# Latent attention scores: two full passes and one of 32 rows for each key half, instead of three full passes

## The chip, the cores and the metric

The kernel runs on one core of a Trainium2 chip. The metric is the device time of the program in microseconds (us); lower is better. Of the kernel before, three runs are given: median 3897.62 us, lowest 3896.55, highest 3898.89.

The core has TensorE (matmuls and transposes, results into the banks of PSUM), VectorE, ScalarE and GpSimd (elementwise work; GpSimd can't reach PSUM here), and SyncE's queue, which issues most DMAs. In the rows PE is TensorE's matmul part, PEld its loading of stationary operands, DVE VectorE, ACT ScalarE, POOL GpSimd, SPq and ACTq the DMA-issuing queues.

## The reference, cut to what matters

The whole program is two transformer blocks in float32 on 1024 tokens: dilated attention, latent attention, then twice a mixer and a gated MLP. The change concerns the latent attention (mixer_mla), 16 heads, 64 channels without and 32 with rotary position:

```
q = (rmsnorm(cq, q_norm) @ w_uq).reshape(B, S, 16, 64 + 32)
q_nope, q_rope = q[..., :64], q[..., 64:]          # q_rope is rotated
kv = (rmsnorm(ckv, kv_norm) @ w_ukv).reshape(B, S, 16, 64 + 64)
k_nope, v = kv[..., :64], kv[..., 64:]             # k_rope is shared by the heads, and rotated
s = (q_nope @ k_nope.T + q_rope @ k_rope.T) * 96 ** -0.5
o = softmax(s) @ v
y = o * silu(gate)
```

## The kernel before, in words

**Precision.** TensorE's fast type for four-byte numbers (fp32r) keeps fewer bits than float32. So an operand x is held as a high part (x rounded to fp32r) and a low part (x minus the high part), and a product is three passes into one bank: high by high, high by low, low by high.

**Layout of a head.** Query and key channels lie on the 128 rows of SBUF, tokens on the 1024 columns. Rows 0 to 63 are the channels without rotary position. The rotation of the query is folded into the product: rows 64 to 95 hold the rotary channels, rows 96 to 127 the same channels with their halves exchanged, and the tile `msh` holds the factors of each row and token (scale, cosines, signed sines). The rotary key stands on rows 64 to 95 and again on 96 to 127, so that the matmul over 128 rows adds both. Buffers: `qh`, `ql` (high and low of the query), `kh`, `kl` (of the key), two of each, for even and odd heads. Rows 64 to 127 of `kh` and `kl` are the same for all heads and are filled once, in the step before (`act_latent`, `dve_latent`).

**The stage.** The heads are computed as 128 units: unit i is head i // 8 and the block i % 8 of 128 queries. Each engine has a written-out program of its own (`pe_heads` L2026, `act_heads` L2078, `dve_heads` L2127, `pool_heads` L1882), in which step i does parts of several units; engines meet only at semaphores, and each works its list strictly in order.

- TensorE, step i: in odd steps two transposes of the gate and 16 matmuls of probabilities by values for a pair of finished units (`bo`); 8 transposes of the probabilities of unit i-3; the scores of unit i; then one piece, if there is one. The scores are two key halves of 512 columns, three passes of 128 rows each, into two banks.
- ScalarE: the exponential with its sum (`act_head_exp`; odd step i: of unit i-1, first; even step: of unit i-1, after the copies), the copy of `bo` to `ml_o`, two copies of the transposed probabilities (high part), and in even steps the pieces of steps i-1 and i.
- VectorE: the sum into `ml_o`, two subtractions (low part of the probabilities, `ml_p`), the row maximum of unit i, the reciprocal of unit i-2, and in even steps the pieces.
- GpSimd: the low part of the query pieces (odd steps), the splitting of weight tiles into high and low (`split`: one CAST, one subtraction; a head's weights at i % 8 = 0, a tile of the output weights at i % 8 = 4 from step 40 on), the product of `ml_o` and gate (even steps from 6), and last the scaling of the gate by the reciprocal of unit i-3. TensorE's gate transposes of step i wait for the scaling of unit i-4.

**Pieces.** A head's query and key (halves q0, k0, q1, k1 of 512 tokens) are made while the head before is attended: in its steps i % 8 = 0 to 3. For even heads the values of two heads follow at i % 8 = 6 and 7. The pieces of head 0 stand ahead of step 0. A query piece goes: six passes on TensorE (`pe_piece`), the product with `msh` into the single buffer `ml_qs` on VectorE (`dve_piece`), which also frees the bank, rounding to `qh` on ScalarE (`act_piece`), subtraction to `ql` on GpSimd (`pool_piece_lo`). The next product waits until rounding and subtraction of the piece before are done. A key piece: three passes, rounding of rows 0 to 63 on ScalarE, subtraction on VectorE. Pieces and `bo` share two banks in turn (ring `o2`), the transposes have two (`t2`), the scores two pairs (`s2`). The scores of a head wait for both halves of its query's low part.

Line numbers of the trace for these calls are those of the helpers: L130 matmul, L133 transpose, L136 activation, L139 copy (CAST), L142 two-operand arithmetic, L145 arithmetic with a scalar, L153 maximum, L159 reciprocal.

Of the kernel before, what the change touches and what calls it, by code (L numbers as in the profile page):

```python
# [8 lines left out]
F32 = mybir.dt.float32  # L9
# [264 lines left out]
class Kernel:  # L274
# [13 lines left out]
    def layout(self):  # L288
# [95 lines left out]
        self.bjk, self.qg, self.kg = self.msc[:, 384:768], self.msc[:, 0:256], self.msc[:, 256:384]  # L384
# [5 lines left out]
        self.qh, self.ql = [self.thi[:, 2 * i, :] for i in range(2)], [self.thi[:, 2 * i + 1, :] for i in range(2)]  # L390
# [1355 lines left out]
    def act_latent(self, q):  # L1746
# [15 lines left out]
        def out(j):  # L1762
# [6 lines left out]
            q.activation(self.kh[0][64:128, blk(j)], kr, ACT.Copy)  # L1769
            q.activation(self.kh[1][64:128, blk(j)], kr, ACT.Copy)  # L1770
# [38 lines left out]
    def dve_latent(self, q):  # L1809
# [17 lines left out]
        def out(j):  # L1827
# [5 lines left out]
            kr = ps[64:128, b, 384:512]  # L1833
            for i in range(2):
                q.tensor_tensor(self.kl[i][64:128, blk(j)], kr, self.kh[i][64:128, blk(j)].bitcast(F32), ALU.subtract)
# [34 lines left out]
    def sp_heads(self, sp):  # L1870
        uq, ukv = self.I["b_w_uq"][0], self.I["b_w_ukv"][0]
        for h in range(16):
            pieces = []
            for k in range(2):
                r = uq[blk(k), h * 96:h * 96 + 96]
                pieces += [(k * 128, r), (k * 128 + 96, r[:, 80:96]), (k * 128 + 112, r[:, 64:80])]
            pieces.append((256, ukv[:, h * 128:h * 128 + 128]))
            if h % 2 == 0:
                pieces += [(384, ukv[:, h * 128 + 64:h * 128 + 128]), (448, ukv[:, h * 128 + 192:h * 128 + 256])]
            self.load(sp, ("head", h), pieces)  # L1880
# [91 lines left out]
    def act_piece(self, q, h, what, hf):  # L1972
# [3 lines left out]
        if what == "q":  # L1976
# [3 lines left out]
            q.activation(self.qh[x][:, r], self.qs[:], ACT.Copy).then_inc(*S.up("hi", key))  # L1980
        elif what == "k":
# [3 lines left out]
            q.activation(self.kh[x][0:64, r], p[0:64, :], ACT.Copy).then_inc(*S.up("hi", key))  # L1985
# [9 lines left out]
    def dve_piece(self, q, h, what, hf):  # L1995
# [3 lines left out]
        if what == "q":  # L1999
# [5 lines left out]
            q.tensor_tensor(self.qs[:], p, self.msh[:, r], ALU.mult).then_inc(*B.free(key, "evac_v"))  # L2005
# [12 lines left out]
    def pool_piece_lo(self, q, h, what, hf):  # L2018
        if what != "q":
# [3 lines left out]
        q.tensor_tensor(self.ql[x][:, r], self.qs[:], self.qh[x][:, r].bitcast(F32), ALU.subtract).then_inc(  # L2023
            *self.S.up("lo_p", ("hq", h, hf)))

    def pe_heads(self, q):  # L2026
# [3 lines left out]
        for i in range(128 + 4):  # L2030
# [22 lines left out]
            if i < 128:  # L2053
# [9 lines left out]
                for c in range(2):  # L2063
                    o, r = ps[:, b + c, :], half(c)
                    q.matmul(o, self.qh[x][:, blk(j)], self.kh[x][:, r], start=True, stop=False)
                    q.matmul(o, self.qh[x][:, blk(j)], self.kl[x][:, r], start=False, stop=False)
                    ins = q.matmul(o, self.ql[x][:, blk(j)], self.kh[x][:, r], start=False, stop=True)
# [1366 lines left out]
```

## Time and profile before

| | |
|---|---|
| median of three runs | 3897.62 us |
| profiled execution, its span (no other time of it is given) | 3899.6 us |
| TensorE, matmuls | 3734.7 us busy, 96%, 19015 instructions |
| VectorE | 2203.4 us, 57% |
| GpSimd | 1920.5 us, 49% |
| ScalarE | 1471.4 us, 38% |

The busy share of an engine is the sum of its instructions' time over the span; matmuls are pipelined and each is shown for longer than its distance to the next. The stage of the heads lies between about 870 and 1430 us of the span. In a timeline row stand: start (us from the span's start), duration (us, of all instructions that the row merges), engine, line, operation, output tile and input tiles, form, count, and in brackets the idle time of the engine just before, with what ended it. The names: `ml_qs` the query product, `thi` (several buffers under one name) the query's parts or the transposed probabilities' high part, `tfi` or `ml_e` the exponentials, `cst_sm` small statistics.

### The profile page before, as it was taken

What the parts mean: (1) busy time and instruction counts of PE and PEld (TensorE: products, weight loads), DVE (VectorE), ACT (ScalarE), POOL (GpSimd) and SP (SyncE); (2) the same over time, 40 slices, a digit from 0 to 9 for tenths busy, and PEclk for the clock granted to TensorE, in tenths of its full rate; (3) what the DMA queues carried; (4) which work ended last, traced back from release to release, by engine and by line L of the source; (5) the groups of instructions that cost most, each with busy time, mean ns of one, the idle gap of its engine ahead of it and who ended that gap; (6) DMA issues with size and microseconds to landing.
All of it is one profiled execution on the core that took longest, in us unless ns stands there. A gap on an engine that the chain in (4) does not pass through costs nothing.

```text
span 3899.6 us, 49530 instructions
## 1 busy us (share of the span) xinstructions
PE 3734.7 (96%) x19015; PEld 3088.3 (79%) x19015; DVE 2203.4 (57%) x3514; ACT 1471.4 (38%) x2954; POOL 1920.5 (49%) x1675
## 2 busy tenths in 40 slices
PE   6999999899999998999898999999999898999998
PEld 5888887887888877877687888887878587888887
DVE  4425254836777756544648777444444648777533
ACT  3224231326666653226544333222225534333211
POOL 3223223823333327221536888976221526778975
PEclk9999999999999999999899999999999999999999
DMA  5323222320000013110132222544110132222543
GB/s 182 96 83 92 81 67 85 107 78 15 6 12 6 9 37 102 61 30 7 33 131 78 81 84 79 200 145 138 49 36 17 33 125 73 84 84 87 180 161 124
DMA packets 244615, 309.84 MB, mean 79 GB/s; under 512 B 38085, under 2 KB 156245, under 8 KB 244378
## 3 DMA queue, kind: packets, MB, share of 16 engines
q1 hardware_dynamic: 211768, 231.86, 19.1%
q10 hardware_dynamic: 32610, 74.80, 5.5%
q8 instruction: 151, 2.47, 0.3%
q14 instruction: 86, 0.70, 0.1%
HBM read 252.96 MB, written 51.53 MB: 78 GB/s over the span
## 4 chain that ended last, share of the span: by engine, by line
PE 68%; DVE 12%; ACT 3%; issue 3%; POOL 1%; DMA 0%; ACTq 0%; SPq 0%; DVEq 0%; POOLq 0%
PE ps L130 64%; PE ps L133 3%; DVE ml_p L142 3%; DVE cst_sm L153 3%; ACT thi L136 1%; DVE f_ta L150 1%; DVE f_tb L150 1%; ACT ml_o L136 1%; DVE tlo L142 1%; ACT tfi L136 0%; POOL mlo_z L142 0%; DVE cst_sm L150 0%; DVE tfl L142 0%; POOL mix_z L142 0%; DMA wst<-in_w_in 0%
## 5 line engine op out<-in xcount | busy, mean ns | idle before, releaser
L139 POOL CAST whi<-wst 128x512 fp32r<-128x512 f32 (+2 forms) x508 | 423.9, 834 | 1241.2 <-DMA wst<-in_a_w_in 347.9
L142 POOL TENSOR_TENSOR wlo<-wst,whi 128x512 fp32r<-128x512 f32 (+2 forms) x634 | 936.2, 1484 | 40.8
L130 PE MATMUL ps<-whi,thi 128*128 128x512 f32 (+3 forms) x1816 | 710.1, 391 | 28.7 <-DVE tlo L142 10.8
L130 PE MATMUL ps<-whi,tlo 128*128 128x512 f32 (+3 forms) x1816 | 686.2, 378 | 0.0
L130 PE MATMUL ps<-wlo,thi 128*128 128x512 f32 (+3 forms) x1816 | 685.6, 378 | 0.0
L130 PEld LDWEIGHTS ps<-whi,thi 128*128 128x128 f32 x1816 | 345.2, 190 | 90.5 <-DVE tlo L142 11.9
L130 PEld LDWEIGHTS ps<-wlo,thi 128*128 128x128 f32 x1816 | 345.5, 190 | 57.7 <-issue 3.8
L130 PEld LDWEIGHTS ps<-whi,tlo 128*128 128x128 f32 x1816 | 344.6, 190 | 58.3
L130 PE MATMUL ps<-thi,whi 128*128 128x512 f32 x856 | 339.2, 396 | 23.2 <-DVE tlo L142 15.0
L130 PE MATMUL ps<-thi,wlo 128*128 128x512 f32 x856 | 336.0, 392 | 0.0
L130 PE MATMUL ps<-tlo,whi 128*128 128x512 f32 x856 | 335.9, 392 | 0.0
L153 DVE TENSOR_REDUCE cst_sm<-ps 128x1 f32<-128x1024 f32 (+7 forms) x256 | 246.2, 982 | 122.4 <-PE ps L130 122.4
L130 PEld LDWEIGHTS ps<-thi,whi 128*128 128x128 f32 x856 | 162.3, 190 | 60.1 <-issue 12.8
L136 ACT ACTIVATE thi<-ps 128x512 fp32r<-128x512 f32 (+2 forms) x258 | 141.1, 565 | 159.8 <-PE ps L133 154.9
L130 PE MATMUL ps<-mla_kh,thi 128*128 128x512 f32 x512 | 191.4, 414 | 1.9 <-ACT tfi L136 1.9
L150 DVE SCALAR_TENSOR_TENSOR f_tb<-f_ub,tfi,f_tb 128x1024 f32<-128x1024 f32 x88 | 190.7, 2167 | 1.6
L130 PEld LDWEIGHTS ps<-thi,wlo 128*128 128x128 f32 x856 | 162.4, 190 | 34.4
L130 PEld LDWEIGHTS ps<-tlo,whi 128*128 128x128 f32 x856 | 162.5, 190 | 33.0
L136 ACT ACTIVATE whi<-wst 128x512 fp32r<-128x512 f32 x126 | 70.5, 622 | 279.1 <-DVE wst L142 241.3
L142 POOL TENSOR_TENSOR tlo<-tfl,thi 128x512 fp32r<-128x512 f32 x96 | 152.3, 1592 | 6.1 <-ACT thi L136 1.1
L145 POOL TENSOR_SCALAR tfl<-tfl,cst_sm 128x64 f32<-128x64 f32 x128 | 56.7, 443 | 182.3 <-DVE cst_sm L159 176.1
L136 ACT ACTIVATE tfi<-ps,cst_sm 128x1024 f32<-128x1024 f32 (+1 forms) x112 | 119.3, 1066 | 50.2 <-DVE cst_sm L153 50.1
(393 smaller groups left out, 8103.9 us busy)
## 6 DMA issues: line engine op xcount, KB each, us to landing
wst<-in_w_down SPq DMA_DIRECT2D x140, 256.0 KB, 3.3
wst<-in_w_up SPq DMA_DIRECT2D x126, 256.0 KB, 2.9
scr_h<-f_tb SPq DMA_DIRECT2D x44, 512.0 KB, 3.9
wst<-in_w_in SPq DMA_DIRECT2D x80, 256.0 KB, 2.8
da_am<-in_ada_w SPq DMA_DIRECT2D x64, 256.0 KB, 2.7
wst<-in_a_w_in SPq DMA_DIRECT2D x72, 192.0 KB, 2.4
f_T2lw<-scr_h SPq DMA_DIRECT2D x48, 256.0 KB, 3.8
tfl<-scr_h SPq DMA_DIRECT2D x40, 256.0 KB, 3.8
```

The costliest lines, as they stand in the source:

```text
L130: return self.none if self.e is None else self.e.matmul(*a, **k)
L133: return self.none if self.e is None else self.e.transpose(*a)
L136: return self.none if self.e is None else self.e.activation(*a, **k)
L139: return self.none if self.e is None else self.e.tensor_copy(*a)
L142: return self.none if self.e is None else self.e.tensor_tensor(*a)
L145: return self.none if self.e is None else self.e.tensor_scalar(*a)
L150: return self.e.scalar_tensor_tensor(out=out, in0=a, scalar=s, in1=b, op0=o1, op1=o2, **k)
L153: return self.none if self.e is None else self.e.tensor_reduce(*a, **k)
```

## The change

The three products are arranged on fewer rows. A query piece is first summed over its two rotary row groups (rows 96 to 127 onto 64 to 95), so that 96 rows are left. Then, with n for the 64 rows without and r for the 32 rows with rotary position:

- pass 1: `q1` = [high n; low n] by `kh` = [high n; high n], 128 rows;
- pass 2: `q2` = [high n; high r; low r] by `kl` = [low n; high r; high r], 128 rows;
- pass 3: high r by low r of the key (`k3`), 32 rows. Of the first key half it uses rows 64 to 95 of `q2` and `k3`; of the second a copy of the query's rotary rows on rows 0 to 31 (even heads) or 32 to 63 (odd heads), with `k3` on the same rows. These two matmuls are the last of a unit, one behind the other.

For this VectorE gets an addition behind the product of a query piece, ScalarE rounds it twice (to `q1`, 64 rows; to `q2`, 96 rows), GpSimd makes two subtractions and a copy instead of one subtraction, and has waits ahead of them. The key piece's weight columns are loaded twice (one more DMA for each head), and its rounding covers 128 rows. In the step before, the rotary key's high part goes to `kl`, its low part to `k3`. A scratch tile (`bjk`) moves.

```
-            q.activation(self.kh[0][64:128, blk(j)], kr, ACT.Copy)
-            q.activation(self.kh[1][64:128, blk(j)], kr, ACT.Copy)
+            q.activation(self.kl[0][64:128, blk(j)], kr, ACT.Copy)
+            q.activation(self.kl[1][64:128, blk(j)], kr, ACT.Copy)
...
-            for i in range(2):
-                q.tensor_tensor(self.kl[i][64:128, blk(j)], kr, self.kh[i][64:128, blk(j)].bitcast(F32), ALU.subtract)
+            kr, krh = ps[64:96, b, 384:512], self.kl[0][64:96, blk(j)].bitcast(F32)
+            for r in (64,) if j < 4 else (0, 32):
+                q.tensor_tensor(self.k3[r:r + 32, blk(j % 4)], kr, krh, ALU.subtract)
...
-            pieces.append((256, ukv[:, h * 128:h * 128 + 128]))
+            pieces += [(256, ukv[:, h * 128:h * 128 + 64]), (320, ukv[:, h * 128:h * 128 + 64])]
...  (act_piece)
-            q.activation(self.qh[x][:, r], self.qs[:], ACT.Copy).then_inc(*S.up("hi", key))
+            q.activation(self.q1[x][0:64, r], self.qs[0:64, :], ACT.Copy)
+            q.activation(self.q2[x][0:96, r], self.qs[0:96, :], ACT.Copy).then_inc(*S.up("hi", key))
...
-            q.activation(self.kh[x][0:64, r], p[0:64, :], ACT.Copy).then_inc(*S.up("hi", key))
+            q.activation(self.kh[x][:, r], p, ACT.Copy).then_inc(*S.up("hi", key))
...  (dve_piece)
-            q.tensor_tensor(self.qs[:], p, self.msh[:, r], ALU.mult).then_inc(*B.free(key, "evac_v"))
+            q.tensor_tensor(self.qs[:], p, self.msh[:, r], ALU.mult).then_inc(*S.up("v_seq"))
+            q.wait_ge(*S.last("v_seq"))
+            q.tensor_tensor(self.qs[64:96, :], self.qs[64:96, :], self.qs[96:128, :], ALU.add).then_inc(*B.free(key, "evac_v"))
+            q.wait_ge(*S.last("evac_v"))
...  (pool_piece_lo)
-        q.tensor_tensor(self.ql[x][:, r], self.qs[:], self.qh[x][:, r].bitcast(F32), ALU.subtract).then_inc(
-            *self.S.up("lo_p", ("hq", h, hf)))
+        q.wait_ge(*self.S.last("w_lo"))
+        if h or hf:
+            q.wait_ge(*self.S.last("b_gate"))
+        q.tensor_tensor(self.q1[x][64:128, r], self.qs[0:64, :], self.q1[x][0:64, r].bitcast(F32), ALU.subtract).then_inc(
+            *self.S.up("p_seq"))
+        q.wait_ge(*self.S.last("p_seq"))
+        q.tensor_tensor(self.q2[x][96:128, r], self.qs[64:96, :], self.q2[x][64:96, r].bitcast(F32), ALU.subtract).then_inc(
+            *self.S.up("p_seq"))
+        q.wait_ge(*self.S.last("p_seq"))
+        if h == 1 and hf == 0:
+            for j in range(8):
+                q.wait_ge(*self.S.at(f"ld_g{j}"))
+        q.tensor_copy(self.q_third(h)[:, r], self.qs[64:96, :]).then_inc(*self.S.up("lo_p", ("hq", h, hf)))
+        q.wait_ge(*self.S.last("lo_p"))
...  (pe_heads)
-                    q.matmul(o, self.qh[x][:, blk(j)], self.kh[x][:, r], start=True, stop=False)
-                    q.matmul(o, self.qh[x][:, blk(j)], self.kl[x][:, r], start=False, stop=False)
-                    ins = q.matmul(o, self.ql[x][:, blk(j)], self.kh[x][:, r], start=False, stop=True)
+                    q.matmul(o, self.q1[x][:, blk(j)], self.kh[x][:, r], start=True, stop=False)
+                    q.matmul(o, self.q2[x][:, blk(j)], self.kl[x][:, r], start=False, stop=False)
+                q.matmul(ps[:, b, :], self.q2[x][64:96, blk(j)], self.k3[64:96, :], start=False, stop=True)
+                ins = q.matmul(ps[:, b + 1, :], self.q_third(h)[:, blk(j)], self.k3[self.third(h), :], start=False, stop=True)
```

## Rows read from the trace of the kernel before

**Rows 1.** Busy time in a stretch of the stage (PE, PEld, DVE, ACT, POOL; clock).

```profile
1114.00:1148.00 34.00, 33.28 (x224) 29.54 (x224) 24.04 (x42) 22.17 (x43) 12.74 (x18) 1.00 0.01 4
```

**Rows 2.** Groups of instructions, 870 to 1430 us: busy, mean ns, idle before.

```profile
L142 POOL TENSOR_TENSOR thi<-ml_qs,thi 128x512 fp32r<-128x512 f32 x32 | 41.2, 1286 | 161.5 <-ACT thi L136 161.5
...
L142 DVE TENSOR_TENSOR ml_qs<-ps,mod_sh 128x512 f32<-128x512 f32 x32 | 21.7, 678 | 54.1 <-PE ps L130 53.8 <-POOL thi L142 0.3
...
L142 DVE TENSOR_TENSOR mla_kl<-ps,mla_kh 64x512 fp32r<-64x512 f32 x32 | 21.3, 664 | 2.4 <-ACT mla_kh L136 2.4
```

**Rows 3.** Timeline of a pair without pieces in the ring.

```profile
1104.04 0.42 PEld L133 LDWEIGHTS ps<-cst_ident,ml_e 128*128 128x128 f32 x4 [0.56 <-DVE ml_p L142]
...
1106.88 1.21 DVE L153 TENSOR_REDUCE cst_sm<-ps 128x1 f32<-128x1024 f32 x1
...
1108.13 1.12 ACT L136 ACTIVATE tfi<-ps,cst_sm 128x1024 f32<-128x1024 f32 x1 [1.11 <-DVE cst_sm L153]
...
1109.36 0.59 ACT L136 ACTIVATE ml_o<-ps 64x512 f32<-64x512 f32 x1
...
1109.98 0.60 ACT L136 ACTIVATE thi<-ps 128x512 fp32r<-128x512 f32 x1
...
1111.81 1.21 DVE L153 TENSOR_REDUCE cst_sm<-ps 128x1 f32<-128x1024 f32 x1
...
1114.20 1.21 DVE L153 TENSOR_REDUCE cst_sm<-ps 128x1 f32<-128x1024 f32 x1
```

**Rows 4.** Timeline of the pair behind it, with one query piece.

```profile
1115.40 0.68 DVE L142 TENSOR_TENSOR ml_qs<-ps,mod_sh 128x512 f32<-128x512 f32 x1
...
1116.12 0.63 ACT L136 ACTIVATE thi<-ml_qs 128x512 fp32r<-128x512 f32 x1 [1.78 <-DVE ml_qs L142]
...
1116.65 1.10 ACT L136 ACTIVATE tfi<-ps,cst_sm 128x1024 f32<-128x1024 f32 x1
...
1118.49 0.42 DVE L142 TENSOR_TENSOR ml_o<-ps,ml_o 64x256 f32<-64x256 f32 x1 [2.41 <-ACT ml_o L136]
...
1122.75 1.21 DVE L153 TENSOR_REDUCE cst_sm<-ps 128x1 f32<-128x1024 f32 x1
```

**Rows 5.** Timeline of the next pair, with a key and a query piece.

```profile
1127.61 0.61 POOL L139 CAST whi<-wst 128x512 fp32r<-128x512 f32 x1
...
1129.51 1.21 DVE L153 TENSOR_REDUCE cst_sm<-ps 128x1 f32<-128x1024 f32 x1
...
1130.96 0.44 POOL L145 TENSOR_SCALAR tfl<-tfl,cst_sm 128x64 f32<-128x64 f32 x1 [0.39 <-DVE cst_sm L159]
1131.06 0.69 DVE L142 TENSOR_TENSOR ml_p<-ps,thi 128x512 fp32r<-128x512 f32 x1 [0.27 <-ACT thi L136]
...
1132.27 1.21 DVE L153 TENSOR_REDUCE cst_sm<-ps 128x1 f32<-128x1024 f32 x1
```

**Rows 6.** Timeline of a pair with value pieces, ScalarE.

```profile
1142.86 0.59 ACT L136 ACTIVATE ml_o<-ps 64x512 f32<-64x512 f32 x1 [0.41 <-PE ps L130]
```

**Rows 7.** Timelines of TensorE around 64-row pairs, from windows that begin at them.

```profile
1734.93 0.39 PE L130 MATMUL ps<-wlo,thi 128*128 128x512 f32 x1
1735.16 0.39 PE L130 MATMUL ps<-whi,tlo 128*128 128x512 f32 x1
1735.48 0.70 PE L130 MATMUL ps<-c_k,c_q 64*128 64x512 f32 x2
...
1736.01 1.02 PE L130 MATMUL ps<-c_k,c_q 64*128 64x512 f32 x4
...
1736.44 1.02 PE L130 MATMUL ps<-c_k,c_q 64*128 64x512 f32 x4
1737.40 0.29 PE L130 MATMUL ps<-cst_cmask,cst_idb 128*128 128x128 bf16 x2
```

**Rows 8.** Timeline of VectorE, 15 subtractions from SBUF behind the stage.

```profile
1428.75 9.11 DVE L142 TENSOR_TENSOR tlo<-tfl,thi 128x512 fp32r<-128x512 f32 x15
```

**Rows 9.** Timelines of VectorE and TensorE at the start of the stage.

```profile
870.74 0.69 DVE L142 TENSOR_TENSOR ml_qs<-ps,mod_sh 128x512 f32<-128x512 f32 x1 [53.64 <-PE ps L130]
...
877.56 0.45 PE L130 MATMUL ps<-mla_kh,thi 128*128 128x512 f32 x1
```

More of the change, by code:

```diff
@@ L383, in layout @@
         self.btmp = t.new("tmp", [128, 4, 16])
-        self.bjk, self.qg, self.kg = self.msc[:, 384:768], self.msc[:, 0:256], self.msc[:, 256:384]
+        self.bjk = self.place("ml2_jk", [128, 384], F32, mod + 81920)
+        self.qg, self.kg = self.msc[:, 0:256], self.msc[:, 256:384]
         t = Region(self, b + 16384, self.end, "ml3")
@@ L389, in layout @@
         self.qs = self.place("ml5_qs", [128, 512], F32, mod + 8192)
-        self.qh, self.ql = [self.thi[:, 2 * i, :] for i in range(2)], [self.thi[:, 2 * i + 1, :] for i in range(2)]
+        self.q1, self.q2 = [self.thi[:, 2 * i, :] for i in range(2)], [self.thi[:, 2 * i + 1, :] for i in range(2)]
+        self.q3 = self.place("ml5_q3", [128, 1024], F32R, b + 12288)
+        self.k3 = self.place("ml5_k3", [128, 512], F32R, mod + 10240)
         self.bp = [self.tfi[:, 4 + i, :] for i in range(3)] + [last[:]]
@@ L1832, in out @@
                     q.wait_ge(*S.at(f"st{i}", "a"))
-            kr = ps[64:128, b, 384:512]
-            for i in range(2):
-                q.tensor_tensor(self.kl[i][64:128, blk(j)], kr, self.kh[i][64:128, blk(j)].bitcast(F32), ALU.subtract)
+            kr, krh = ps[64:96, b, 384:512], self.kl[0][64:96, blk(j)].bitcast(F32)
+            for r in (64,) if j < 4 else (0, 32):
+                q.tensor_tensor(self.k3[r:r + 32, blk(j % 4)], kr, krh, ALU.subtract)
             q.tensor_tensor(self.cql[:, :, blk(j)], ps[:, b, 0:256].rearrange("p (a b) -> p a b", a=2),
@@ L2022, in pool_piece_lo, with third, q_third @@
         q.wait_ge(*self.S.at("hi", key))
-        q.tensor_tensor(self.ql[x][:, r], self.qs[:], self.qh[x][:, r].bitcast(F32), ALU.subtract).then_inc(
-            *self.S.up("lo_p", ("hq", h, hf)))
+        q.wait_ge(*self.S.last("w_lo"))
[12 more added lines that the diff above has]
+        q.wait_ge(*self.S.last("lo_p"))
+    def third(self, h):
+        return slice(32 * (h % 2), 32 * (h % 2) + 32)
+    def q_third(self, h):
+        return (self.q3 if h else self.thi[:, 7, :])[self.third(h), :]
     def pe_heads(self, q):
```

## The prediction, made before the changed kernel was run

> **What bounds the kernel now.** I read the page's busy shares first, then the granted clock, then the timeline of the attention heads, one unit (head and block of 128 queries) after another. The page says TensorE: 96% busy over the span, and 33.28 of 34 us in a stretch of that stage, with the upper of its two clock levels, 2.4 GHz, granted throughout (1.00) [rows 1]. The order of the work in the stage says otherwise. It has 128 units; the program goes through them in pairs, an even unit, then an odd one, and the start of the even unit's row maximum on VectorE marks a pair. Read by these marks, the eight pairs of two heads take 9.60, 9.54, 7.32, 7.32, 8.56, 9.53, 7.32 and 9.13 us, 68.3 in all, repeating to 0.02 us from head 2 to head 14; the 7.32, 8.56 and 9.53 can be taken from the marks in [rows 3 to 5].
>
> In a pair without pieces (7.32) the marks are 1106.88 and 1114.20 [rows 3]. Between them: maximum, exponential on ScalarE at 1108.13, copy of the output (ml_o) at 1109.36, copy of the transposed probabilities (thi) at 1109.98, two VectorE subtractions, the odd maximum at 1111.81, two more subtractions, the next mark. No step waits for TensorE; it is a ring of VectorE and ScalarE. TensorE waits for it instead: 0.56 us at 1104.04, for the subtraction that frees its bank. A shorter score block makes such waits longer, no more.
>
> In a pair with one query piece (8.56 = 7.32 + 1.24) the piece lies in the same ring: ml_qs on VectorE at 1115.40, its rounding on ScalarE at 1116.12, and only then, in ScalarE's order, the exponential at 1116.65 [rows 4]. In pairs with key and query piece it is the same ring, plus 0.38 us in which the second subtraction pair comes late behind TensorE (ScalarE's copy, then 0.27 us of VectorE wait at 1131.06; maximum to maximum 2.76 instead of 2.39) [rows 5]. Only the pair with value pieces (9.13) has TensorE ahead of ml_o [rows 6].
>
> **The change, part by part.**
>
> *TensorE, scores.* Per unit six passes of 512 columns become four and a pair of 32-row passes on disjoint rows, into two banks. Pitch of such a pass: 1735.16 - 1734.93 = 0.23 us [rows 7]. No 32-row pair is in the trace. The nearest are the 64-row pairs of the differential attention: two matmuls that both start at 1735.48 have ended 0.70 us later, and the next two start at 1736.01, where one after the other each would take the 0.43 between 1736.01 and 1736.44 [rows 7]: they run side by side. (These are of another type, 0.43 and not 0.23 us a pass.) I take the new pair as one pass. But those rows also show a price. From the last full-height matmul to the first pair it is 0.32 us instead of 0.23 (+0.09); from the first pair to the second 0.53 instead of 0.43 (+0.10); and 1736.44 to 1737.40, two pairs and the way back to full height, is 0.96 instead of 0.86 (+0.10). Sum: -0.23 + 0.09 + 0.10 + 0.10 = +0.06 us a unit; with a little for a slow first matmul behind it, +0.1 is my value, bounds -0.23 (no price) and +0.33 (no overlap, with the price). In the pair without pieces the last score pass ends as late as before (a step of 0.09 more, 0.23 less, a pass 0.1 longer), so the ring keeps its 7.32. With the value pieces two units count: 7 pairs x 0.2 = +1.4 us (bounds -3.2 and +4.6).
>
> The Trainium skill ("TensorEngine Tiling (Array Packing)", Key Properties) says that a change of tiling mode drains TensorE; its page "TensorE: Matmul & The Clock Gate", Measured speedup vs the span model, gives packed tiles a matmul's duration and about 4 ns for each further tile. The trace agrees with both: side by side, at a price on each side. By the second rule alone the scores would save a pass a unit, the value pairs would gain 3.2 us where I count a loss of 1.4, and the sum below would be 40.
>
> *VectorE and ScalarE, query piece.* After the multiplication VectorE now waits for itself and adds rows 96 to 127 onto rows 64 to 95, and only then releases ScalarE, which rounds twice (64 and 96 rows) instead of once. Fewer rows don't shorten these (kl's 64 rows take 0.66 us, ml_qs's 128 take 0.68) [rows 2]. The add: 512 elements from SBUF on VectorE take 9.11/15 = 0.61 us in a row of 15 [rows 8]; alone, with its start and the self-wait before it, I take 0.70. The second rounding: ScalarE's step from rounding to exponential, 1116.65 - 1116.12 = 0.53 [rows 4]. Together +1.23 us ahead of the exponential, in the ring: bounds 1.1 (0.61 and 0.5) and 1.4 (0.75 and 0.65). There are 32 pieces [rows 2], 30 inside the stage. Seven are alone in their pair: 7 x 1.23 = 8.6. Two in the first head, unpaced by TensorE: 2.5. In the other 21 the 0.38 us of lateness goes, as TensorE is then early: 21 x 0.85 = 17.9. Sum 29.0. What is late next is still the ring; ml_qs is single, but its next user comes 7 us later.
>
> *GpSimd, query piece.* One subtraction of 1.29 us [rows 2] becomes two and a copy of 0.61 (the CAST of rows 5), with self-waits: 3.4 us, +2.1, and starts later by the ring's 1.23. In most pairs GpSimd has over 2 us of waiting to absorb it. Behind the second query piece of a head, however, comes in 10 heads the splitting of an output weight tile (1127.61, then 1.3 us), then ml_o's product, and then the scaling of the gate at 1130.96 for which TensorE's next transposes wait. Laid out: piece 1127.15 to 1130.5, gate, split to 1132.85, product to 1133.7, gate scaled at 1134.15; TensorE would be there at 1132.85. It then ends the value products 2.3 us later, at 1136.5, where ml_o could begin at 1135.6. So 10 x 0.9 = 9 us (bounds 0 and 12).
>
> *Start of the stage.* The first head's pieces have no cover. Now ml_qs at 870.74, first scores at 877.56 [rows 9]. After, with the durations above: product and sum 1.4 us, two roundings to 873.2, GpSimd 3.4 us to 876.7, then the second ml_qs (which waits for GpSimd), rounding to 879.2, GpSimd to 882.65. Scores at 882.7: +5.1 us (bounds 2 and 8; a fall of the clock in TensorE's new idle time is in the upper one).
>
> *At nothing:* the key piece's copy of 128 rows for 64 (same duration); fewer subtractions in the latent step, under TensorE's gate matmuls; one more DMA a head on SP's queue, loaded two heads ahead; GpSimd's wait for the gate DMAs at head 1, issued 15 us before. Without their cover they are under a us each. No other stage changes.
>
> Sum: 29.0 + 1.4 + 9 + 5.1 = +44.5. The profiled execution has no own time beside its span of 3899.6; the median of the runs is 2.0 lower. 3899.6 + 44.5 - 2.0 = 3942. As the GpSimd term is the least sure of a laid-out chain, I take it at half: 3938.
>
> **Rivals.**
> (a) *TensorE is the bound, as its 96% say*: each unit saves a pass, 128 x 0.23 = 29 us: 3868, faster. For it: the page, and 2.76 against 2.39 in 21 pairs. Against it: the ring's rows, in which no step of a 7.32 pair waits for TensorE. It decides only if the ring had slack that the rows don't show. Chance 0.06.
> (b) *The additions hide*: VectorE's wait of 2.41 us before ml_o's sum [rows 4] takes them up, TensorE is a wash, the start costs its 2 to 5: about 3900. Against it: that wait is for ScalarE, whose queue holds the rounding and the exponential, the ring itself. Chance 0.07.
> (c) *Ring lengthened, GpSimd and start absorbed*: 29.0 + 1.4 + 2: 3930. Same sign; chance 0.27.
> (d) *The 32-row passes don't overlap* (the promised saving doesn't come): +0.33 us a unit. Score ends then pass VectorE's readiness by about 0.2 in the odd-even step of 64 pairs, +13, and the value pairs +4.6: 44.5 + 13 + 3: 3958. Against it [rows 7]. Chance 0.12.
>
> **How the numbers follow.** The forecast (all terms, GpSimd in part to whole: 3932 to 3950) has 0.48; likeliest time 3938. A measurement of this kernel tells 0.2%, 7.8 us, from no change. The range leaves out (a), (b) and the far end of (d): 3912 to 3958. Faster: (a) and a little of (b), 0.07. Within: most of (b), 0.05. Slower: 0.88.
>
> **What would show it.** Marks of pairs without pieces still 7.32 apart; of the lone query pair 9.8; of key and query pairs 10.4 with the odd-even step at 2.39. Between ml_qs and the exponential 2.5 us instead of 1.25. The two 32-row passes start within 0.01 us, with 0.32 before them. TensorE's waits in the stage grow, although its busy time falls. A GpSimd wait of over 1 us before the value products in heads 5 to 14. First scores 5 us later after the first ml_qs. The forecast is wrong if the pairs without pieces get shorter than 7.32, or if the query pairs stay at 8.56.

## The result, and the profile after

The changed kernel takes 3949.4 us (median of 4 runs, 3947.2 to 3952.0) where the kernel before takes 3898.3 beside it: a ratio of 1.0133, interval 1.0120 to 1.0145. That is 51 us slower; the forecast was 3938, the range 3912 to 3958. The direction and the range held. The sum behind them did not hold in three of its terms.

The head of the page after (engine, busy us, share of the span, instructions):

```profile
span 3945.4 us, 49752 instructions
PE 3758.3 (95%) x19015; PEld 3052.3 (77%) x19015; DVE 2236.7 (57%) x3542; ACT 1490.9 (38%) x2986; POOL 1976.6 (50%) x1739
```

Busy time in the stage, from the first query product to the last row maximum; first line the kernel before, second the kernel after (stretch, its length, then PE, PEld, DVE, ACT, POOL with instruction counts; clock; DMA):

```profile
870.74:1414.29 543.55, 520.82 (x3362) 449.40 (x3360) 386.19 (x661) 363.51 (x663) 185.60 (x269) 1.00 0.04 11
```

```profile
868.74:1470.24 601.50, 555.82 (x3362) 423.03 (x3360) 406.64 (x693) 383.02 (x695) 246.40 (x333) 0.98 0.04 10
```

The stage is 58.0 us longer. TensorE issues the same 3362 matmuls in it; the time in which none ran goes from 22.7 to 45.7 us. Its busy time grew too, by 35 us: the scores of a unit take it 0.18 us longer (shown below), which is 23 us in 128 units, and part of the stage runs at the lower clock level (0.98 on the mean).

Groups of the stage after that answer to [rows 2] (line, engine, operation, tiles, form, count; busy us, mean ns; idle time before and its cause):

```profile
L142 POOL TENSOR_TENSOR thi<-ml_qs,thi 64x512 fp32r<-64x512 f32 x32 | 41.1, 1283 | 202.2 <-ACT thi L136 202.2
L142 POOL TENSOR_TENSOR thi<-ml_qs,thi 32x512 fp32r<-32x512 f32 x32 | 41.0, 1282 | 2.5
L142 DVE TENSOR_TENSOR ml_qs<-ml_qs 32x512 f32<-32x512 f32 x32 | 22.0, 686 | 1.1
L139 POOL CAST ml_q<-ml_qs 32x512 fp32r<-32x512 f32 x30 | 18.1, 602 | 2.0
```

Fewer rows cost the same: 1283 ns for 64, 1282 for 32, 1286 for 128 in [rows 2].

The timeline of a lone query piece after, which answers to [rows 4] (start, duration, engine, line, operation, tiles, form, count, idle time before):

```profile
1141.61 1.21 DVE L153 TENSOR_REDUCE cst_sm<-ps 128x1 f32<-128x1024 f32 x1
...
1143.01 0.69 DVE L142 TENSOR_TENSOR ml_qs<-ps,mod_sh 128x512 f32<-128x512 f32 x1
...
1143.73 0.69 DVE L142 TENSOR_TENSOR ml_qs<-ml_qs 32x512 f32<-32x512 f32 x1
...
1144.45 1.15 ACT L136 ACTIVATE thi<-ml_qs 64x512 fp32r<-64x512 f32 x2 [2.70 <-DVE ml_qs L142]
...
1145.51 1.10 ACT L136 ACTIVATE tfi<-ps,cst_sm 128x1024 f32<-128x1024 f32 x1
1145.69 2.66 POOL L142 TENSOR_TENSOR thi<-ml_qs,thi 64x512 fp32r<-64x512 f32 x2 [4.56 <-ACT thi L136]
...
1147.42 0.42 DVE L142 TENSOR_TENSOR ml_o<-ps,ml_o 64x256 f32<-64x256 f32 x1 [3.00 <-ACT ml_o L136]
...
1151.56 1.21 DVE L153 TENSOR_REDUCE cst_sm<-ps 128x1 f32<-128x1024 f32 x1
```

From the product to the exponential it is 2.50 us (1145.51 - 1143.01) where [rows 4] have 1.25. The maxima are 9.95 apart.

TensorE around a 32-row pair after, which answers to [rows 7]:

```profile
1140.55 0.40 PE L130 MATMUL ps<-mla_kl,thi 128*128 128x512 f32 x1
1140.88 0.50 PE L130 MATMUL ps<-ml_k,thi 32*128 32x512 f32 x1
1140.88 0.50 PE L130 MATMUL ps<-ml_k,ml_q 32*128 32x512 f32 x1
1141.31 0.50 PE L130 MATMUL ps<-mla_cqh,whi 128*128 128x512 f32 x1
1141.65 0.39 PE L130 MATMUL ps<-mla_cql,whi 128*128 128x512 f32 x1
```

Both matmuls of the pair start together. The steps are 0.33 before the pair, 0.43 behind it and 0.34 behind the first full matmul, 1.10 in all from the last full pass to normal pace (1140.55 to 1141.65), where four steps of 0.23 would be 0.92. So a unit costs TensorE 0.18 us more than six full passes, not less. In the 128 units the median steps are 0.33 and 0.43 too.

Marks (even units' maxima, as the prediction reads them) in both kernels. The last column is the difference over the stage. The pairs are named here by what VectorE's list has in them, which sets two names of the prediction right: the 9.60 pairs, seven of its 21 "key and query" pairs, have a value and a query piece, and 15 of the 26 pairs of 7.32 us that it calls "without pieces" have a key piece, which leaves them at 7.32 all the same.

| pair of units | before | after | in all |
|---|---|---|---|
| first product to fourth maximum | 21.53 | 34.60 | +13.1 |
| lone query piece, 7 pairs | 8.56 | 9.95 | +9.8 |
| key and query piece, 14 pairs; value and query piece, 7 pairs | 9.53; 9.60 | 10.33; 10.39 | +16.7 |
| value piece alone, 7 pairs | 9.13 | 9.46 | +2.4 |
| key piece alone, with the output weight's split, 10 pairs (heads 5 to 14) | 7.32 | 8.65, two of them 10.0 | +16.0 |
| other pairs with a key piece alone or none | 7.32 | 7.32 | 0 |

Sum 58.0, the stage's 58.0. The rest of the program is 12 us shorter in the profiled execution, and 7 if the stage's 58.0 is set against the medians' 51.1.

Two readings of the kernel before belong beside this table. In its lone query pair (8.56) TensorE is busy for 8.55 of 8.55 us:

```profile
1114.20:1122.75 8.55, 8.55 (x56) 7.58 (x55) 5.93 (x12) 5.38 (x11) 2.89 (x4) 1.00 0.00 0
```

The same holds for its value pairs. In a key and query pair (9.53) TensorE waits once, for VectorE's subtraction of the key piece:

```profile
1056.38 0.44 PE L133 MATMUL ps<-cst_ident,tfl 128*128 128x128 f32 x2 [0.62 <-DVE mla_kl L142]
```

### The profile page after: what moved, and what is told of

Its sections match the earlier page's. It is cut to its first block, busy times and chain, and to the rows that moved or that the text cites. A ratio compares the mean times of both kernels' runs of the same rounds, so it can differ in the third digit from the quotient of the medians.

```text
span 3945.4 us, 49752 instructions
## 1 busy us (share of the span) xinstructions
PE 3758.3 (95%) x19015; PEld 3052.3 (77%) x19015; DVE 2236.7 (57%) x3542; ACT 1490.9 (38%) x2986; POOL 1976.6 (50%) x1739
## 4 chain that ended last, share of the span: by engine, by line
PE 76%; DVE 12%; ACT 5%; issue 3%; POOL 3%; DMA 1%; SPq 0%; ACTq 0%; POOLq 0%; DVEq 0%
PE ps L130 72%; PE ps L133 4%; DVE ml_p L142 3%; DVE cst_sm L153 2%; ACT thi L136 2%; DVE ml_qs L142 1%; ACT tfi L136 1%; ACT ml_o L136 1%; DMA tfi<-in_ada_w 1%; DVE f_ta L150 1%; DVE tlo L142 1%; DVE f_tb L150 0%; POOL thi L142 0%; POOL wlo L142 0%; POOL mlo_z L142 0%
## 5 line engine op out<-in xcount | busy, mean ns | idle before, releaser
L130 PEld LDWEIGHTS ps<-thi,whi 128*128 128x128 f32 x856 | 162.2, 190 | 58.6 <-issue 12.9
L142 POOL TENSOR_TENSOR thi<-ml_qs,thi 64x512 fp32r<-64x512 f32 x64 | 82.1, 1282 | 204.7 <-ACT thi L136 202.2
L150 DVE SCALAR_TENSOR_TENSOR f_ta<-f_ua,tfi,f_ta 128x1024 f32<-128x1024 f32 x88 | 138.6, 1575 | 4.8 <-ACT f_ta L136 3.1
```

Source lines behind the costliest of these rows:

```text
L130: return self.none if self.e is None else self.e.matmul(*a, **k)
L142: return self.none if self.e is None else self.e.tensor_tensor(*a)
L150: return self.e.scalar_tensor_tensor(out=out, in0=a, scalar=s, in1=b, op0=o1, op1=o2, **k)
```

## The experiments

### The parts one by one

**e1_pass**: the kernel before with the third pass as a 32-row pair (the rest of the third product is left out) and nothing else changed.

```
-                    ins = q.matmul(o, self.ql[x][:, blk(j)], self.kh[x][:, r], start=False, stop=True)
+                for c in range(2):
+                    g = slice(64 * (1 - c), 64 * (1 - c) + 32)
+                    ins = q.matmul(ps[:, b + c, :], self.ql[x][g, blk(j)], self.kh[x][g, half(c)], start=False, stop=True)
```

> The kernel before with the new form of the score passes alone: four passes of 128 rows and, as third product, a 32-row pass for each key half on disjoint rows (64 to 95 and 0 to 31), from the old buffers; the rest of the third product is left out. No added work on VectorE, ScalarE or GpSimd. Theory (the stage is a ring of VectorE and ScalarE, and the 32-row pair costs TensorE more than the pass it saves): pairs without pieces stay at 7.32 us, value pairs 9.13 to about 9.4, in all +2 to +5 us. Rival (TensorE is the bound and the added query work ate the gain): about -29 us, pairs shortened by 0.46.

Measured: ratio 1.0025 (1.0014 to 1.0036), +8.7 us, more than the 2 to 5 expected. The 7.32 pairs stay, value pairs go to 9.46, lone query pairs to 8.91, key and query pairs to 9.70. So the saving claimed for TensorE isn't there even alone. Its price of 0.18 us a unit lands in full, 0.35 a pair, where TensorE was busy throughout (value pairs and lone query pairs), and by 0.17 in the other query pairs. Prediction and expectation had counted it only in value pairs. No run leaves the third pass out altogether, so what a pass that is really saved would give stays unmeasured.

**e2_ring**: the kernel before with a second VectorE operation behind the product (a maximum of 32 rows with themselves) and the rounding in two halves.

```
+            q.wait_ge(*S.last("v_seq"))
+            q.tensor_tensor(self.qs[96:128, :], self.qs[96:128, :], self.qs[96:128, :], ALU.max).then_inc(*B.free(key, "evac_v"))
...
-            q.activation(self.qh[x][:, r], self.qs[:], ACT.Copy).then_inc(*S.up("hi", key))
+            q.activation(self.qh[x][0:64, r], self.qs[0:64, :], ACT.Copy)
+            q.activation(self.qh[x][64:128, r], self.qs[64:128, :], ACT.Copy).then_inc(*S.up("hi", key))
```

> The kernel before with the query piece's additions on VectorE and ScalarE alone: behind the product a 32-row, 512-column operation in place that leaves the values as they are (maximum with itself) with its self-waits, and the rounding in two instructions of 64 rows. Scores and GpSimd as before. Theory: +1.25 us in each of 30 query pieces, of which 0.38 to 0.45 is covered in 21: +29 us, and 2.5 at the start: +31. Lone query pair 8.56 to 9.8, key and query pairs 9.53 to 10.33. Rival (the loss is mainly TensorE's, through mode changes in 128 units): under +10.

Measured: 1.0100 (1.0085 to 1.0115), +38.9 us. Lone query pairs 10.02, key and query pairs 10.59 (value and query 10.66), and the start, to the fourth maximum, 31.50 instead of 21.53: 10 us of the 38.9. Its two roundings take longer than those of the change:

```profile
1148.63 0.67 DVE L142 TENSOR_TENSOR ml_qs<-ps,mod_sh 128x512 f32<-128x512 f32 x1
1149.34 0.69 DVE L142 TENSOR_TENSOR ml_qs<-ml_qs 32x512 f32<-32x512 f32 x1
1150.06 1.27 ACT L136 ACTIVATE thi<-ml_qs 64x512 fp32r<-64x512 f32 x2 [2.61 <-DVE ml_qs L142]
1151.36 1.12 ACT L136 ACTIVATE tfi<-ps,cst_sm 128x1024 f32<-128x1024 f32 x1
```

1.30 us from rounding to exponential (1150.06 to 1151.36), 1.06 after the change (1144.45 to 1145.51). By this 0.24 a piece, 7 us over 30 pieces, the ring's part of the change, with its part of the start, is about 32, an estimate. It is the main part.

**e3_pool**: the kernel before with GpSimd's work of a query piece as in the change: a copy and two subtractions instead of one subtraction, with their waits.

```
+        q.tensor_copy(self.ql[x][64:96, r], self.qs[64:96, :]).then_inc(*self.S.up("p_seq"))
...
+        q.tensor_tensor(self.ql[x][0:64, r], self.qs[0:64, :], self.qh[x][0:64, r].bitcast(F32), ALU.subtract).then_inc(
...
+        q.tensor_tensor(self.ql[x][64:128, r], self.qs[64:128, :], self.qh[x][64:128, r].bitcast(F32), ALU.subtract).then_inc(
```

> The kernel before with GpSimd's additions alone: a copy of 32 rows and two subtractions of 64 rows instead of one of 128, with the waits for itself. Theory: the start of the stage +4 us, and in 10 heads the gate's scaling behind the output weight's splitting comes late, by 0.5 us on the ring (less than the 1.33 in the changed kernel, since GpSimd starts 1.25 us earlier here): about +9 us. Rival (GpSimd's waiting of over 2 us absorbs all of it): 0 to +2.

Measured: 1.0037 (1.0024 to 1.0050), +13.7 us. The ten pairs go from 7.32 to 8.20, the others stay, and the start grows by 5.8 us (21.53 to 27.29). The expectation had 0.5 for the ten pairs. That 0.88 is near the prediction's 0.9 is luck, since the prediction's figure stands for the whole change, where the ring's additions delay GpSimd too and 1.33 came.

The three parts alone give 61 us, 54 without e2's dearer roundings, against 51: they add nearly up.

### GpSimd's late gate

**e4_late_split**: the kernel after with the splitting of the output weight tile behind the scaling of the gate.

```
-            if i % 8 == 4 and 40 <= i < 128:
-                self.split(q, ("wo", "b", n // 8, n % 8))
...  (scaling of the gate)
+            if i % 8 == 4 and 40 <= i < 128:
+                self.split(q, ("wo", "b", n // 8, n % 8))
```

> The changed kernel with the splitting of the output weight tile moved behind the gate's scaling in GpSimd's step. Theory: the ten pairs of 8.65 and 10.0 us fall back to 7.32, 16 us of the changed kernel's loss go: +35 against the kernel before. Rival (those pairs are late for another reason, a transfer or VectorE): no change, +51.

Measured: 1.0098 (1.0083 to 1.0113), 3936.5 us, 12.9 less than the kernel after, and 16.2 less in the stage. All ten pairs are at 7.32 again, every other pair as after. This is what it removes, in the kernel after:

```profile
1159.42 0.45 POOL L145 TENSOR_SCALAR tfl<-tfl,cst_sm 128x64 f32<-128x64 f32 x1
...
1159.81 0.61 POOL L139 CAST whi<-wst 128x512 fp32r<-128x512 f32 x1
...
1160.51 1.29 POOL L142 TENSOR_TENSOR wlo<-wst,whi 128x512 fp32r<-128x512 f32 x1
...
1161.97 0.73 POOL L142 TENSOR_TENSOR tfl<-ml_o 64x256 f32<-64x256 f32 x1 [0.17 <-DVE ml_p L142]
...
1162.79 0.92 POOL L145 TENSOR_SCALAR tfl<-tfl,cst_sm 128x64 f32<-128x64 f32 x2
...
1163.29 0.44 PE L133 MATMUL ps<-cst_ident,tfl 128*128 128x128 f32 x2 [1.63 <-POOL tfl L145]
...
1164.05 0.34 PE L130 MATMUL ps<-thi,ml_v 128*128 128x256 f32 x1
1164.19 0.41 PE L130 MATMUL ps<-ml_p,ml_v 128*128 128x256 f32 x1
1164.40 0.42 PE L130 MATMUL ps<-thi,ml_v 128*128 128x256 f32 x1
```

The scaling that the gate's transposes need stands behind the split and the product in GpSimd's list; TensorE waits 1.63 us. In this pair (10.0 us) something follows: the value products step 0.12 us apart until 1164.05 and 0.21 from 1164.19 on. The granted clock, by stretches, here and in one of the eight pairs of 8.65:

```profile
1160.00:1163.00 3.00, 1.66 (x9) 0.89 (x7) 3.00 (x5) 2.52 (x5) 2.65 (x4) 1.00 0.02 5
1163.00:1168.00 5.00, 4.71 (x27) 4.71 (x28) 1.18 (x4) 2.17 (x4) 0.78 (x3) 0.66 0.00 0
1203.00:1208.00 5.00, 4.37 (x32) 3.82 (x32) 2.21 (x6) 2.89 (x5) 1.67 (x4) 1.00 0.01 3
```

After the wait the clock went to its lower level of 1.2 GHz for a while, and the pair's further 1.35 us go with that. In all ten pairs TensorE waits 1.63 to 1.66 us before the gate's transposes; in the eight others the clock stayed at 2.4 GHz, and why these two and not those is open. The Trainium skill ("TensorE: Matmul & The Clock Gate", HAM oscillation — how this bites in real kernels) tells of long waits for DMA between bursts of matmuls, each of which throttles the PE again. Here the wait is for GpSimd and of 1.65 us, and the lower level followed in two of ten places, so a wait of this length does it sometimes and not always.

### Is there one ring or two

**e5_exp_first**: the kernel before with ScalarE's rounding of the query piece behind the exponential, and the late split.

```
+            if i % 2 == 1 and self.piece_at(i - 1) and self.piece_at(i - 1)[1] == "q":
+                self.act_piece(q, *self.piece_at(i - 1))
...
-                    if self.piece_at(n):
+                    if self.piece_at(n) and self.piece_at(n)[1] != "q":
```

> The kernel before with two moves of order and no change of the work: ScalarE rounds the query piece behind the copies of the next odd step, so behind the exponential instead of ahead of it, and GpSimd splits the output weight tile behind the gate's scaling. Theory (the query piece lies in the ring only because of ScalarE's order): it leaves the ring; query pairs fall from 8.56 and 9.53 to what TensorE needs, about 7.9 and 8.5; pairs without pieces stay 7.32. In all about -25 us, 3874. Rival (TensorE or another engine holds the query pairs just as tightly): under 5 us of gain.

Measured: 0.9994 (0.9984 to 1.0003), 3896.7 us. No gain in the pairs: 9.53 stays 9.53, the lone pairs stay at 8.53 to 8.57, and 14 pairs with a key piece alone go from 7.32 to 7.50. The start falls by 4.0 us (21.53 to 17.51), of which those 14 take back 2.5. The theory of a single ring through the query piece fell. In the lone pairs TensorE has no idle time, as in the kernel before, so it holds them by itself. What is late in a key and query pair of e5:

```profile
1115.84 1.22 DVE L153 TENSOR_REDUCE cst_sm<-ps 128x1 f32<-128x1024 f32 x1
...
1117.04 0.66 DVE L142 TENSOR_TENSOR mla_kl<-ps,mla_kh 64x512 fp32r<-64x512 f32 x1
1117.09 1.11 ACT L136 ACTIVATE tfi<-ps,cst_sm 128x1024 f32<-128x1024 f32 x1 [0.44 <-DVE cst_sm L153]
...
1117.76 0.44 PE L133 MATMUL ps<-cst_ident,tfl 128*128 128x128 f32 x2 [0.62 <-DVE mla_kl L142]
...
1120.15 0.60 ACT L136 ACTIVATE ml_o<-ps 64x512 f32<-64x512 f32 x1 [1.86 <-PE ps L130]
```

The exponential is early, at 1117.09, and of no use: ScalarE then waits 1.86 us for TensorE's value products, which waited 0.62 for VectorE's key subtraction to free the bank. This second ring (maximum, key piece, bank, value products, ml_o) is what holds the pair at 9.53; in the 9.60 pairs the value piece stands in the key piece's place.

**e6_exp_first_after**: the same edit on the kernel after.

> The changed kernel with the same two moves. Theory: its added 1.25 us for each query piece leave the ring too; query pairs 8.2 and 8.8 instead of 9.95 and 10.33, unless GpSimd's longer piece (3.3 us) delays the gate's scaling; with the start's loss of some 10 us left, -35 to -45 us against the changed kernel with the late splitting: about 3897 (3890 to 3910), so near the kernel before and some 20 us behind the kernel before with the moves. Rival (with the query work out of the ring the saved pass pays): below the kernel before with the moves.

Measured: 1.0216 (1.0201 to 1.0231), 3984.8 us, 88 us above the 3897 expected, and slower than e4 (3936.5) instead of faster. GpSimd's piece of 3.3 us now begins 4.94 us behind the query product (1155.87 to 1160.81 of its trace), and 6.22 behind the next (1165.19 to 1171.41), where the kernel after has 2.68 (1143.01 to 1145.69). The next gate scaling and the next query product wait for it, and the 15 pairs behind a head's second query piece grow from 7.32 to between 10.8 and 12.6. Part of that is the clock: it is 0.94 on the mean of the stage here, 0.99 in e4. A step that left one engine's path was still on another's.

**e7_exp_first_pass**: e5 with the 32-row pair of e1.

> The kernel before with the two moves and the new form of the score passes alone (four full passes and the 32-row pair; the rest of the third product is left out). Here TensorE is the bound in the pairs with pieces, so it is the place where a saved pass would pay most. Theory: the pair costs TensorE 0.18 us a unit more than the two passes it replaces: 62 units in 31 pairs, +11 us against the kernel before with the moves. Rival (the pair saves 0.23 us a unit where TensorE is the bound): -14 us against it.

Measured: 1.0013 (1.0004 to 1.0022), 3904.8 us, +8.1 on e5 where 11 were expected. The pairs with pieces are those of e1 to 0.02 us (8.92, 9.70, 9.78, 9.46): the 32-row pair costs the same with the other order. TensorE is idle in the key and query pairs, so the expectation's premise that it is the bound holds for the lone query and value pairs only.

**e8_serial**: e1 with both 32-row matmuls on rows 64 to 95, so that they can't run side by side.

```
-                    g = slice(64 * (1 - c), 64 * (1 - c) + 32)
+                    g = slice(64, 96)
```

> The kernel before with four full passes and two 32-row passes on the same rows (64 to 95) for both key halves, so that they can't lie side by side (the rest of the third product is left out). Theory (the pair on disjoint rows overlaps fully): 0.23 us a unit more than on disjoint rows, +14 us in the 31 pairs with pieces and some +5 in the others through late scores: about +28 us against the kernel before. Rival (the price in the pair is not overlap but the 32-row form itself): the same as on disjoint rows, +9.

Measured: 1.0061 (1.0046 to 1.0076), +25.9 us, 17 more than e1. Here the pair is 0.66 us from start to the next matmul (1100.83 to 1101.49 below) instead of 0.43:

```profile
1100.50 0.40 PE L130 MATMUL ps<-mla_kl,thi 128*128 128x512 f32 x1
1100.83 0.73 PE L130 MATMUL ps<-mla_kh,thi 32*128 32x512 f32 x2
1101.49 0.50 PE L130 MATMUL ps<-mla_cqh,whi 128*128 128x512 f32 x1
```

So the overlap of the change is real and worth one pass, 0.23 us a unit; the steps into and out of the 32-row form stay. This is the prediction's case (d), which it priced at 16 us above its own sum; here it is 17.

**e9_no_sum**: e4 without VectorE's sum. The rotary part of rows 96 to 127 is left out of the query.

```
...
-            q.wait_ge(*S.last("v_seq"))
-            q.tensor_tensor(self.qs[64:96, :], self.qs[64:96, :], self.qs[96:128, :], ALU.add).then_inc(*B.free(key, "evac_v"))
```

> The kernel after, with the output-weight split behind the gate scaling (as in e4_late_split), and without VectorE's sum of the two 32-row parts: the low part of rows 96 to 127 of the query is left out, and the gathering reads what is there. Theory: the sum (0.69 us of VectorE between the query sum and the two roundings) stands on the chain of each pair with a lone query piece, so those pairs fall by about 0.7 us (9.95 to 9.2); pairs with a key and a query piece fall less, since a second ring of the same pair (the maximum, the key piece on VectorE, the bank, the value products, their division) ends at about 9.7, so 10.33 to 9.7; with the start's five pieces this makes about -22 us against e4_late_split: 3914. Rival: the sum lies in time VectorE waits anyway; then all pairs stay and the time is that of e4_late_split, 3936.

Measured: 1.0052 (1.0037 to 1.0068), 3916.6 us. Lone query pairs 9.23 (from 9.95), key and query pairs 9.70 (from 10.33), the start 4.6 us less. The sum is on the path for its full 0.72 in the first, and in the second for 0.63, down to the 9.70 that e1 has without any of the ring's additions: the second ring's length with the 32-row pair in it.

**e10_k_first**: the kernel before with the key piece brought forward, on ScalarE ahead of the even step's exponential, on VectorE ahead of the maximum.

```
+                if self.piece_at(i - 1) and self.piece_at(i - 1)[1] == "k":
+                    self.act_piece(q, *self.piece_at(i - 1))
...  (dve_heads, ahead of the maximum)
+            if i % 2 == 0 and self.piece_at(i - 1) and self.piece_at(i - 1)[1] == "k":
+                self.dve_piece(q, *self.piece_at(i - 1))
```

> The kernel before, with the key piece's work brought forward alone: ScalarE rounds the key piece before the even step's exponential and VectorE subtracts it before the maximum; the query piece as before. Theory of two rings of nearly equal length in a pair with key and query piece (9.53 us): the second (maximum, key piece, bank, value products, division) is cut and the first (query sum, rounding, exponential, value products, division, next query sum) holds at about 9.15: 21 pairs by about -0.4, -8 us: 3891. Rival: one ring only, that of the query; then nothing falls, or the earlier key rounding delays the exponential and the time grows by up to 12 us.

Measured: 1.0010 (1.0001 to 1.0019), 3900.1 us where 3891 was expected, a miss on the whole. The pairs that had 9.53 fall to 9.09, near the 9.15 expected. So the two rings of that pair aren't quite equal: the second is 9.53, the first about 9.1. But each key piece now lies in the pair before: the 9.60 become 10.20 and the lone query pairs 9.15, which I had not counted (the 9.53 pairs lose one key piece and get the next), and two heads take 68.6 us instead of 68.3. The start grows by 1.2.

**e11_k_exp_first**: e10 and e5 together, both rings cut.

> The kernel before, with both rings cut: the key piece brought forward as in e10_k_first, and the query piece rounded behind the exponential with the output-weight split moved back as in e5_exp_first. Theory of two rings: each cut alone gives nothing or little, both together give what neither does: pairs with both pieces from 9.53 to about 8.9, lone query pairs 8.55 as they are, 21 pairs by about 0.6: -13 us, 3885. Rival: a third wait (the division's bank, or TensorE's own work) stands right behind; then under 3 us is gained.

Measured: 0.9982 (0.9974 to 0.9991), 3888.7 us beside 3896.3: 7.6 us, the one version faster than both kernels, by about as little as can be told. The pairs with 9.53 go to 8.71. Neither cut alone did that (9.53 in e5, 9.09 in e10). TensorE's wait for the key's subtraction is gone; what is left is 0.32 us for the gate:

```profile
1123.30 1.10 ACT L136 ACTIVATE ml_e<-ps,cst_sm 128x1024 f32<-128x1024 f32 x1
...
1123.69 0.67 DVE L142 TENSOR_TENSOR mla_kl<-ps,mla_kh 64x512 fp32r<-64x512 f32 x1
...
1123.96 0.44 PE L133 MATMUL ps<-cst_ident,tfl 128*128 128x128 f32 x2 [0.32 <-POOL tfl L145]
...
1124.29 1.20 DVE L153 TENSOR_REDUCE cst_sm<-ps 128x1 f32<-128x1024 f32 x1
```

The pairs that got the key pieces give back most of it (9.60 to 10.20, 8.56 to 9.15): over the pairs of the stage 2.7 us are left. The start gains another 4.0 us, and that is the same 4.0 that e5 has alone. So the pairs show both rings, but the 7.6 us of the whole are only in smaller part theirs.

### The start

**e12_keep_clock**: e4 with 37 unused matmuls of 512 columns among the first head's pieces.

```
+            n = {("q", 0): 2, ("k", 0): 4, ("q", 1): 3, ("k", 1): 12, ("v", 0): 4, ("v", 1): 12}[piece[1:]]
...
+            for k in range(n):
+                q.matmul(ps[:, b0, :], self.cqh[:, 0, blk(0)], self.cqh[:, 0, half(0)], start=True, stop=True)
```

> The kernel after with the output-weight split behind the gate scaling (as e4_late_split), and 37 matmuls of 512 columns whose result nobody reads, put among the first head's pieces so that TensorE is not left idle there. Theory: the granted clock at the start of the scores (0.50 to 0.74 in windows of 5 us between 875 and 900 us in the kernel after, 1.00 in the kernel before) falls because TensorE waited for the first pieces, and costs some 3 to 5 us; with TensorE kept busy the clock reads 1.00 and the time from the first query sum to the fourth reduction goes from 34.6 to about 31, the whole from 3936 to about 3932. Rival: the start's loss is the chain of pieces alone; then the stretch stays at 34.6 or grows by what the added matmuls delay.

Measured: 1.0105 (1.0091 to 1.0119), 3937.0 us, as e4, where 3932 was expected. The clock over the start (the number behind the five engines' busy times), first in the kernel after, then in e12:

```profile
875.00:880.00 5.00, 3.10 (x18) 2.91 (x19) 2.62 (x5) 2.29 (x5) 2.37 (x2) 0.74 0.29 53
880.00:885.00 5.00, 5.00 (x16) 3.56 (x16) 1.63 (x3) 0.66 (x2) 2.66 (x4) 0.50 0.25 43
885.00:890.00 5.00, 4.57 (x14) 2.87 (x12) 2.94 (x4) 1.56 (x3) 0.35 (x1) 0.74 0.27 53
```

```profile
880.00:885.00 5.00, 5.00 (x23) 3.70 (x22) 1.71 (x3) 0.58 (x2) 2.36 (x3) 1.00 0.29 53
885.00:890.00 5.00, 2.82 (x12) 1.58 (x10) 2.87 (x4) 2.90 (x4) 1.62 (x2) 1.00 0.28 54
890.00:895.00 5.00, 4.21 (x10) 2.63 (x11) 1.33 (x3) 2.33 (x5) 1.50 (x2) 0.54 0.00 0
```

The clock holds until 890 us; but between 885 and 890 TensorE is idle for 2.2 of 5 us, and behind that it falls. First product to fourth maximum is 33.7 us instead of 34.6; the first maximum came 0.35 later, the three maxima behind it took 1.3 less. The trace's clock records have the lower level for 7 us of this stretch in e12 and for 17 in e4 and in the kernel after. So the fall was put off and made shorter, not taken away: 10 us less of it gave back 1.3 us. What the rest of it costs stays open.

## Why the prediction was right or wrong, step by step

- *The ring, query piece* (8.6 and 17.9 forecast, 9.8 and 16.7 measured): right in its additions, half right in what held the pairs before. Product to exponential is 2.50 us, the forecast's 2.5. The sum takes 0.72 (0.70 taken), the second rounding 0.53 (0.53). The lone pair rose by 1.40, not 1.23: the product stands 1.40 behind the maximum (1141.61 to 1143.01) and not 1.20 (1114.20 to 1115.40 in [rows 3, 4]), because TensorE ends the piece later: its own price reaching the ring. The forecast read the lone pair of the kernel before as the ring of VectorE and ScalarE alone. It was a tie: TensorE is never idle in it and e1, which lengthens TensorE's work alone, lengthens it by 0.35, while e2's 10.02 less its additions of 1.48 gives 8.54 for the ring (an estimate). That the additions came in full is owed to this tie. Key and query pairs rose by 0.80 (0.85 forecast). That they rise by less than the lone ones was put down to 0.38 us in which the second subtractions come late behind TensorE; e5, e9, e10 and e11 show behind it a second ring, through the key piece and the bank, which held the pair at 9.53 while the ring of the query piece was about 9.1. The sizes fit: e10's 9.09 and the additions of 1.25 make 10.34 (10.33 measured), with e2's 1.48 it is 10.57 (10.59 measured). The number was right, its reason was half of the truth, and it matters: a cut in the query piece's ring (e5) gained nothing in any pair.
- *TensorE, the pair* (1.4 forecast): right in kind, too low in size. Taken +0.1 us a unit, measured +0.18: the step behind the pair is 0.43 us and the next again 0.34, so both the entry and the exit are paid behind the 0.33 ahead. In [rows 7] the exit showed as 0.10 only. Value pairs 2.4 us instead of 1.4, and in e1 another 6 us in the query pairs and the start, which the forecast had at nothing. Pairs without pieces 7.32, as said.
- *Marks of waiting*: TensorE's waits grew, as said; that its busy time falls was wrong, it rose by 35 us in the stage, 23 of them the 0.18 us in each of 128 units.
- *GpSimd*: the mechanism and its place were right, the size was not. 10 x 0.9, taken at half "as the least sure of a laid-out chain", measured 16.0. Alone, in e3, it is 0.88 a pair. With the ring's and TensorE's additions, GpSimd starts later and it is 1.33, and two pairs pay 1.35 more, with the lower clock in them. The laid-out chain was 0.4 a pair short, and halving it doubled that miss.
- *Start*: 5.1 us to the first scores, measured 5.8 (868.74 to the scores at 881.34; 6.82 before). But from the first scores to the fourth maximum another 7.3 are lost where 2.5 were counted, in a stretch with a clock of 0.50 to 0.74, which had been named only as an upper bound. Sum of both 13.1, forecast 7.6. e2 alone has 10.0 of them and e3 alone 5.8, so the additions cost more here than the forecast's chain has; how much of that is the clock, e12 leaves open.
- *All other stages at nothing*: the stage's 58.0 against 44.5 would have been 13 us too low. The program outside it got 12 us shorter in the profiled execution, 7 by the medians. No edit explains it: of the experiments' profiled executions the part behind the stage lies between 2479.6 and 2487.1 us, that of the kernel after at 2475.1, that of before at 2485.3. The clock is the likely cause: behind the stage the trace's clock records have the lower level for 108 us in all in the kernel before and for 81 in the kernel after (88 to 113 in the experiments), and over these 14 executions the part behind the stage is longer where that sum is larger (correlation 0.83). No run sets the clock there, so it isn't shown. That the whole came out at 51 and not 58 is luck, and it made the forecast look better than its terms were.
- *Rivals*: (a) fell: e1 gives +8.7 where it wanted -29, since no pass is saved; TensorE did hold the value pairs, as the forecast says, and the lone query pairs in a tie with the ring, which it doesn't say. (b) fell: VectorE's wait ahead of ml_o grew from 2.41 to 3.00 and took up nothing (e2, e9). (c) fell: GpSimd and the start weren't absorbed (e3, e4). (d) fell: the two matmuls start together, and e8 shows what it would have cost.

## What to carry to other kernels

Time on an engine that waits for others is worth nothing (0.18 us a unit more left the 7.32 pairs as they were), and a change of the array's form has a price on both sides of it that can eat the pass: read the steps from start to start, into the short matmuls, out of them, and one further. What pays for such a saving (a sum, a second rounding, a longer low part) is to be followed on each engine's ordered list to the wait that ends next; here all three were paid nearly in full. Where two rings are nearly equal in length, cutting the shorter shows nothing (e5) and cutting the longer only their difference (0.44 us a pair in e10); both must be cut in one experiment, with the work that was moved counted where it lands.

## What the runs showed of the hardware

- Two 32-row matmuls on different rows start 0.003 us apart. Among full-height passes, 0.23 us apart, the step into the pair costs 0.10 us more than that, the step out of it 0.20 and the one behind the first full matmul 0.11, in all more than the pass that the pair saves. On the same rows the two start 0.34 us apart (e8).
- Two roundings of ScalarE on rows 0 to 63 and 0 to 95 take 1.06 us from the first's start to the next instruction, on rows 0 to 63 and 64 to 127 1.30 (e2). Why is open.
- Rows don't matter for these operations of VectorE and GpSimd: 32 rows of 512 columns take VectorE 0.69 us and GpSimd 1.28, 128 rows 0.68 and 1.29.
- A wait of TensorE of 1.63 to 1.66 us was followed by the lower clock level in two of ten like places.
